# Top-k experts of a transformer layer: row gathers replaced by dense products over all 16384 experts

## What is computed

```
q = (h @ w_pq).reshape(n, 8, 2, 128)
s1 = einsum('nhd,hkd->nhk', q[:, :, 0], pk1)      # 128 keys per head
s2 = einsum('nhd,hkd->nhk', q[:, :, 1], pk2)
v1, i1 = top_k(s1, 16); v2, i2 = top_k(s2, 16)
cand = v1[..., :, None] + v2[..., None, :]        # best 16 of the 256 sums
cidx = i1[..., :, None] * 128 + i2[..., None, :]
sc, j = top_k(cand, 16); e = take_along_axis(cidx, j)
g = softmax(sc)
a = gelu(einsum('nhkd,nd->nhk', pu[e], h))        # pu, pv: [16384, 1024]
y = einsum('nhk,nhkd->nd', g * a, pv[e])
out = layer_norm(2 ** 0.25 * h + y)
```

## Time and profile before

| what | value |
|---|---|
| median of 3 runs | 4867.93 us (4850.75 to 4873.79) |
| span of the profiled execution | 4854.9 us |
| VectorE, TensorE, GpSimd, ScalarE busy | 2587.8, 3808.4, 2443.7, 821.8 us |
| software queue (the gathers) | 1107.96 MB, its packets 61.2% of 16 engines' span |
| hardware queue (all other loads and stores) | 74.99 MB, 5.1% |
| written to HBM | 6.20 MB |

### The profile page before, as it was taken

One profiled execution on the slowest core, in us unless ns is written; L12 is line 12 of the kernel. 1 busy time (PEld: TensorE's weight loads), 2 busy tenths in 40 slices (PEclk: granted clock), 3 DMA queues, 4 the chain that ended last, 5 costly groups with the idle time before them and its releaser, 6 DMA issues.

```text
span 4854.9 us, 35025 instructions
## 1 busy us (share of the span) xinstructions
PE 3808.4 (78%) x10196; PEld 1735.7 (36%) x10196; DVE 2587.8 (53%) x5932; ACT 821.8 (17%) x1886; POOL 2443.7 (50%) x2256
## 2 busy tenths in 40 slices
PE   9899898878999667888676667677778667667677
PEld 4444445545664523333222222223234222222222
DVE  0323239997214675666565465465556656445453
ACT  1210123332100111111111111111111111111111
POOL 0000000000000077777777777777777777777776
PEclk9889989987799889999999999999999999999999
DMA  2100100000210499999999999999999999999998
GB/s 82 36 2 2 55 19 20 14 7 1 70 35 27 128 340 347 354 333 332 355 364 363 366 367 360 367 372 362 362 364 388 352 355 355 359 359 353 352 368 320
DMA packets 405562, 1185.00 MB, mean 244 GB/s; under 512 B 39936, under 2 KB 125248, under 8 KB 405264
## 3 DMA queue, kind: packets, MB, share of 16 engines
q0 software_dynamic: 304384, 1107.96, 61.2%
q1 hardware_dynamic: 101008, 74.99, 5.1%
HBM read 1176.60 MB, written 6.20 MB: 244 GB/s over the span
## 4 chain that ended last, share of the span: by engine, by line
POOL 20%; DMA 17%; PE 15%; issue 9%; DVE 5%; ACT 1%; POOLq 0%; DVEq 0%; SPq 0%; ACTq 0%
DMA v_rows<-in_pv,v_rows_at 14%; PE acc L1412 11%; POOL u_rows L1351 10%; POOL v_rows L1357 9%; PE pq_ps L1379 4%; DMA u_rows<-in_pu,u_rows_at 2%; DVE u_rows L1614 1%; PE key_ps L1387 0%; DVE key_at L1507 0%; DVE one_hot L1600 0%; ACT diag L1461 0%; DVE one_hot L1596 0%; DVE key_top L1504 0%; DVE top_at L1507 0%; DVE expert_f L1602 0%
## 5 line engine op out<-in xcount | busy, mean ns | idle before, releaser
L1412 PE MATMUL acc<-v_rows,diag 128*128 128x512 f32 (+1 forms) x4224 | 2064.5, 623 | 840.6 <-DMA v_rows<-in_pv,v_rows_at 587.5
L1614 DVE CUSTOM_DVE_ANT_0 u_rows<-u_rows,late 128x1024 f32<-128x1024 f32 x1056 | 1274.2, 1226 | 1061.5 <-DMA u_rows<-in_pu,u_rows_at 1054.7
L1412 PEld LDWEIGHTS acc<-v_rows,diag 128*128 128x128 f32 (+1 forms) x4224 | 751.2, 192 | 2135.1 <-issue 1261.4
L1357 POOL DMA_INDIRECT v_rows<-in_pv,v_rows_at x1056 | 1225.1, 1160 | 325.3 <-issue 235.8
L1351 POOL DMA_INDIRECT u_rows<-in_pu,u_rows_at x1056 | 1179.8, 1117 | 369.9 <-issue 291.3
L1461 ACT ACTIVATE diag<-ident_sb,expert_w 128x128 f32<-128x128 f32 x1024 | 379.7, 397 | 1451.4 <-PE acc L1412 1364.6
L1338 POOL COPY u_rows_at<-expert 128x16 uint32<-128x16 uint32 (+1 forms) x66 | 20.2, 306 | 1193.2 <-DVE expert L1605 1180.8
L1379 PE MATMUL pq_ps<-xT_sb,w_pq_sb 128*128 128x256 f32 (+2 forms) x768 | 238.8, 465 | 8.2 <-DMA iota_sb<-in_iota 7.6
L306 POOL DMA_DIRECT2D out_gla_p<-gla_S x4 | 2.3, 587 | 480.9 <-DVE gla_S L630 480.9
L1504 DVE MAX8 key_top<-key_scores 128x8 f32<-128x128 f32 (+1 forms) x288 | 68.1, 283 | 271.2 <-ACT key_scores L1447 171.3
L930 DVE MAX8 m<-score 128x8 f32<-128x384 f32 (+6 forms) x209 | 183.4, 878 | 5.3
(11 more groups left out here) (207 smaller groups left out, 3045.9 us busy)
## 6 DMA issues: line engine op xcount, KB each, us to landing
w_pq_sb<-in_w_pq SPq DMA_DIRECT2D x48, 512.0 KB, 12.6
u_rows<-in_pu,u_rows_at POOLq DMA_INDIRECT x1056, 6.2
v_rows<-in_pv,v_rows_at POOLq DMA_INDIRECT x1056, 6.2
xT_sb<-in_xT SPq DMA_DIRECT2D x8, 528.0 KB, 7.0
w_gvr<-in_w_in SPq DMA_DIRECT2D x2, 2048.0 KB, 13.0
w_gk<-in_w_in SPq DMA_DIRECT2D x8, 512.0 KB, 6.1
w_dsa<-in_w_in SPq DMA_DIRECT2D x2, 2048.0 KB, 10.3
w_b<-in_w_in SPq DMA_DIRECT2D x8, 512.0 KB, 4.2
```

The source lines that it names most:

```text
L1357: pool.indirect_dma_start(out=V[:, j % RING, :], out_offset=None, in_=io["pv"], in_offset=bass.IndirectOffsetOnAxis(ap=atv[:, b, j:j + 1], ...
L1412: last = pe.matmul(acc[0:R, c * 512:(c + 1) * 512], dg[:, j % DG, 0:R], V[:, j % RING, c * 512:(c + 1) * 512], start=False, stop=False)
L1614: dve.tensor_tensor_reduce(U[:, j % RING, :], U[:, j % RING, :], h1[:, t, :], 1.0, 0.0, ALU.mult, ALU.add, dots[:, b, j:j + 1]).then_inc(d ...
```

## The change

`run_experts` no longer gathers. It goes over all 16384 experts for all tokens, in two passes with two scratch tensors in DRAM between them, both in float32: `gelu_rows` (128 blocks x 128 experts x 1056 tokens) and `weight_rows` (33 groups of 32 tokens x 128 x 4096). Each has 69 MB.

Pass 1 runs over 128 blocks of 128 experts. SP loads a block of `pu` in one piece (`load_block`, three buffers, each free again when TensorE has transposed it). TensorE transposes it in two halves (`turn`), ScalarE copies the halves out of PSUM, TensorE multiplies with `h1T` in three thirds of 352 tokens (`product`), ScalarE applies the gelu out of PSUM, and SP stores the 540 KB. Blocks 0 to 15 also make the queries of all tokens, one pair of head and half at a time (`query`), and blocks 1 to 16 the key scores (`keys`); VectorE takes the best 16 of all nine tiles beside that. After the picks of tile 0, block 22 transposes its numbers and weights (`turn_chosen`), so that the 128 picks of a token lie on partitions. From block 24 on, three "quads" of four tokens go beside each block, up to block 111: for each token GpSimd compares an iota with the first key numbers (`hot_key1`), VectorE with the second ones and multiplies by the weight (`hot_key2`), and TensorE multiplies the two 128x128 matrices (`weights`). That gives the token's weights of all experts; ScalarE copies four tokens at a time into one of two halves of `stage`, which SP stores as 2 MB every eight quads. The picks of the next tile go between the quads on VectorE. `early` is one SBUF buffer that holds the query data first and `stage` later.

Pass 2 is a block of its own, 32 groups of four U blocks. SP loads the gelus (`coef`), the weights (`weight_in`, in pieces of 512 bytes) and `pv`; VectorE multiplies the first two; TensorE multiplies the product with V, eight matmuls of 512 columns for each of nine tiles; VectorE adds the result to `h1` in SBUF. In the last group each tile is normalized after its add and stored by SP.

```diff
-    RING = 8
-    DG = 4
-    MAIN = TILES - 1
-    GROUPS = [[0, 1], [2, 3, 4, 5], [6, 7, 8]]
+    EB = NEXP // P
+    TC = [(0, 352), (352, 704), (704, 1056)]
+    QUADS = [r // 4 for r in ROWS]
+    NQ = sum(QUADS)
+    QAT = [sum(QUADS[:t]) for t in range(TILES)]
+    NG = NT // 32
+    KT = [[0, 1, 2, 3], [4, 5, 6, 7], [8]]
+    FIRST = 24
+    gelu_rows = nc.dram_tensor("gelu_rows", (EB, P, NT), F32, kind="Internal").ap()
+    weight_rows = nc.dram_tensor("weight_rows", (NG, P, P * 32), F32, kind="Internal").ap()
+    def quads_beside(c):
+        return [q for q in range(3 * (c - FIRST), 3 * (c - FIRST) + 3) if 0 <= q < NQ]
...
+        early = sb("early", [P, 2 * P * 32 + 512])
...
-        U = sb("u_rows", [P, RING, D])
-        V = sb("v_rows", [P, RING, D])
...
+                load_block(0)
+                load_query(0)
                 sp.dma_start(pk[:], io["pkT"]).then_inc(pk_in, 16)
                 sp.dma_start(iota[:], io["iota"]).then_inc(pk_in, 16)
...
+                load_block(1)
+                load_query(1)
+                stored = 0
+                for c in range(EB):
+                    if c + 2 < EB:
+                        load_block(c + 2)
+                    if 1 <= c and c + 1 < NB:
+                        load_query(c + 1)
+                    if c >= 1:
+                        sp.wait_ge(gelu_done, 3 * c)
+                        sp.dma_start(gelu_rows[c - 1], ga[:, (c - 1) % 3, :]).then_inc(ga_out[(c - 1) % 3], 16)
+                    while stored < NG and 8 * stored + 8 <= 3 * (c - 1 - FIRST):
+                        sp.wait_ge(w_copied, 8 * (stored + 1))
+                        sp.dma_start(weight_rows[stored], stage[:, stored % 2].rearrange("p c n -> p (c n)")).then_inc(stage_out[stored % 2], 16)
+                        stored += 1
...
+                def turn(c, half):
+                    if half == 0:
+                        pe.wait_ge(pu_in[c % 3], 16 * (c // 3 + 1))
+                    if c:
+                        pe.wait_ge(turned_copied, 2 * (c - 1) + half + 1)
+                    for b in range(4):
+                        last = pe.transpose(tps[:, half, b * P:(b + 1) * P], pu[:, c % 3, (4 * half + b) * P:(4 * half + b + 1) * P], ident[:])
+                    last.then_inc(turned, 1)
+                def product(c, s):
+                    n, (a, b) = 3 * c + s, TC[s]
+                    if s == 0:
+                        pe.wait_ge(turned_copied, 2 * c + 2)
+                    if n >= 2:
+                        pe.wait_ge(gelu_done, n - 1)
+                    for kk in range(KD):
+                        last = pe.matmul(sps[:, n % 2, 0:b - a], puT[:, c % 2, kk, :], h1T[:, kk, a:b], start=(kk == 0), stop=(kk == KD - 1))
+                    last.then_inc(s_ready, 1)
...
+                def weights(q):
+                    pe.wait_ge(hot1_built, q + 1)
+                    pe.wait_ge(hot2_built, q + 1)
+                    if q >= 2:
+                        pe.wait_ge(w_copied, q - 1)
+                    for x in range(4):
+                        last = pe.matmul(gps[:, q % 2, x * P:(x + 1) * P], oh2[:, q % 4, x, :], oh1[:, q % 4, x, :], start=True, stop=True)
+                    last.then_inc(w_ready, 1)
+                turn(0, 0)
+                turn(0, 1)
+                for c in range(EB):
+                    if c + 1 < EB:
+                        turn(c + 1, 0)
+                    if c == FIRST - 2:
+                        turn_chosen(0)
+                    for s in range(3):
+                        if c < NB:
+                            query(c, s)
+                        if 1 <= c <= NB:
+                            keys(c - 1, s)
+                        product(c, s)
+                        if s == 0 and c + 1 < EB:
+                            turn(c + 1, 1)
+                        for q in quads_beside(c)[s:s + 1]:
+                            weights(q)
+                            t = tile_of(q)
+                            if t + 1 < TILES and q == QAT[t] + 28:
+                                turn_chosen(t + 1)
+                def gelu(c, s):
+                    n, (a, b) = 3 * c + s, TC[s]
+                    act.wait_ge(s_ready, n + 1)
+                    if c >= 3 and s == 0:
+                        act.wait_ge(ga_out[c % 3], 16 * (c // 3))
+                    act.activation(ga[:, c % 3, a:b], sps[:, n % 2, 0:b - a], ACT.Gelu).then_inc(gelu_done, 1)
...
+                def copy_weights(q):
+                    k = q // 8
+                    act.wait_ge(w_ready, q + 1)
+                    if k >= 2 and q % 8 == 0:
+                        act.wait_ge(stage_out[k % 2], 16 * (k // 2))
+                    act.copy(stage[:, k % 2, :, 4 * (q % 8):4 * (q % 8) + 4],
+                             gps[:, q % 2, :].rearrange("p (x c) -> p c x", x=4)).then_inc(w_copied, 1)
...
-                            pool.indirect_dma_start(out=U[:, j % RING, :], out_offset=None, in_=io["pu"],
-                                                    in_offset=bass.IndirectOffsetOnAxis(ap=atu[:, b, j:j + 1], axis=0)).then_inc(u_in[j % RING], 16)
...
-                            pool.indirect_dma_start(out=V[:, j % RING, :], out_offset=None, in_=io["pv"],
-                                                    in_offset=bass.IndirectOffsetOnAxis(ap=atv[:, b, j:j + 1], axis=0)).then_inc(v_in[j % RING], 16)
...
+                pool.iota(count[:], [[1, P]], base=0, channel_multiplier=0, allow_small_or_imprecise_dtypes=True).then_inc(counted, 1)
+                pool.wait_ge(counted, 1)
+                for t in range(TILES):
+                    pool.wait_ge(sel_copied, t + 1)
+                    for q in range(QAT[t], QAT[t] + QUADS[t]):
+                        if q >= 4:
+                            pool.wait_ge(w_ready, q - 3)
+                        for x in range(4):
+                            n = 4 * (q - QAT[t]) + x
+                            last = pool.tensor_scalar(oh1[:, q % 4, x, :], count[:], selT[:, t % 2, 0, n:n + 1], None, ALU.is_equal)
+                        last.then_inc(hot1_built, 1)
...
-                        dve.tensor_tensor_reduce(U[:, j % RING, :], U[:, j % RING, :], h1[:, t, :], 1.0, 0.0, ALU.mult, ALU.add,
-                                                 dots[:, b, j:j + 1]).then_inc(dot_done, 1)
...
+                def hot_quad(t, q):
+                    if q >= 4:
+                        dve.wait_ge(w_ready, q - 3)
+                    for x in range(4):
+                        n = 4 * (q - QAT[t]) + x
+                        last = dve.tensor_scalar(oh2[:, q % 4, x, :], count[:], selT[:, t % 2, 1, n:n + 1], selT[:, t % 2, 2, n:n + 1],
+                                                 ALU.is_equal, ALU.mult)
+                    last.then_inc(hot2_built, 1)
+                for b in range(NB):
+                    dve.wait_ge(k_copied, 3 * (b + 1))
+                    top16(lambda x: v[:, x, b, :], lambda x: iu[:, x, b, :], lambda x: kw[:, b % 2, x, :], SAMPLE)
+                    top16(lambda x: v[0:TS, SAMPLE, b, :], lambda x: iu[0:TS, SAMPLE, b, :], lambda x: kw[0:TS, b % 2, SAMPLE, :], 1)
+                    link.wait()
+                    dve.sem_inc(top_done, 1)
+                for part in range(PH + 2):
+                    pick(0, part)
+                for t in range(TILES):
+                    dve.wait_ge(sel_copied, t + 1)
+                    for q in range(QAT[t], QAT[t] + QUADS[t]):
+                        hot_quad(t, q)
+                        part, left = divmod(q - QAT[t], 2)
+                        if t + 1 < TILES and left == 1 and part <= PH:
+                            pick(t + 1, part)
+                        if t + 1 < TILES and q == QAT[t] + 24:
+                            pick(t + 1, PH + 1)
+    GRP = EB // 4
...
+        ca = sb("coef", [P, 3, 4, NT])
+        wt = sb("weight_in", [P, 2, NG, 4, 32])
+        V = sb("pv_sb", [P, 3, 4, D])
...
+                for g in range(GRP):
+                    if g >= 3:
+                        sp.wait_ge(o_ready, TILES * (g - 2))
+                    sp.dma_start(ca[:, g % 3], gav[g]).then_inc(ca_in[g % 3], 16)
+                    if g >= 2:
+                        sp.wait_ge(c_ready, 4 * (g - 1))
+                    sp.dma_start(wt[:, g % 2].rearrange("p k c n -> p k (c n)"), wtv[g]).then_inc(wt_in[g % 2], 16)
+                    sp.dma_start(V[:, g % 3], pvv[g]).then_inc(V_in[g % 3], 16)
+                    if g == 1:
+                        sp.dma_start(gain, io["ln2_g"].to_broadcast([P, D])).then_inc(ln_in, 16)
+                        sp.dma_start(offset, io["ln2_b"].to_broadcast([P, D])).then_inc(ln_in, 16)
...
+            @block.tensor
+            def _(pe):
+                for g in range(GRP):
+                    pe.wait_ge(c_ready, 4 * (g + 1))
+                    pe.wait_ge(V_in[g % 3], 16 * (g // 3 + 1))
+                    for t in range(TILES):
```

(56 more changed lines are left out.)

551 lines of the change are left out of this document (198 added, 353 removed).

## The result

The changed kernel takes 6074.57 us (median of 4 runs, 6064.53 to 6085.92), the kernel before 4868.31 in the same comparison (4850.75 to 4873.79). The ratio is 1.2476, with an interval of 1.2438 to 1.2513. The forecast was 3970, faster, with a range to 4200. It was wrong by 2100 us and on the wrong side.

A forecast was written before the change was run, and what follows sets the result against it. It took the old expert stage as bound by gather bytes and the new one by PE: start 1602.4, pass 1 to 2907, turnover 23, 31 groups 958, last group 63.7, end 2.4, 13 outside the span: 3970 µs, range 3910 to 4200.

The forecast's parts named there:

- the price of a matmul: PE in both passes: 24 matmuls of 352 columns 7.10 µs, 32 of 512 columns 13.74; PE's floor 2257 µs.
- the charge of 20: Pass 1: 20 µs together (0 to 60) for POOL and DVE locking, the `stage` margin and nine ACT function table exchanges.
- That TensorE paces both passes: Both passes: PE work of 1267.9 µs and 989 µs sets the time; PE over 95% busy from 1602 to the turnover.
- Stores run like loads: Pass 1 DMA: 199 GB/s is covered if stores reach the rate of loads, 376 GB/s in 4 KB rows.
- Rival 3: Scratch stores pace pass 1: 4015 µs at 200 GB/s, 4755 at 79; chance 0.10 together with slow reads.
- The strided weight copy on ACT: Pass 1, three per block: no row shows it; 2.2 µs each would fill the block, so nothing was charged.
- Turnover: Between pass 1 and pass 2: last gelu, its store, first loads and four products leave PE idle for 23 µs.
- Clock after a wait: PE at 1.2 GHz for a part: 2 µs each at the start, after block 22 and at pass 2, 6 together.
- Stall at block 22: Pass 1: PE waits at `turn_chosen(0)` for DVE's picks of the first tile, 13 µs (0 to 20).
- Tail: Last group of pass 2: DVE adds and normalizes nine tiles at 6.70 µs each, 63.7 in all, twice PE's time.
- POOL's price: Pass 1, `hot_key1`: 0.3 µs for each of 1056 `tensor_scalar` of 128 elements; POOL paces quads only above 0.77.
- POOL beside DVE: Pass 1 quads: POOL loses up to one DVE operation per issue, at worst 6.2 of 6.2 µs per two quads.

The follow-up runs named there:

- `half_all`: The changed kernel with half of the U products, half of the query products and half of pass 2's products left out: 4100.02 us.
- `uv_bf16`: The changed kernel with the products of both passes in bfloat16; queries, keys and one-hot products stay float32: 3426.1 us, timed 3433.14, ratio 0.7048 to the kernel before.

## Why the prediction was wrong, step by step

**The step that failed: the price of a matmul.** The forecast put "24 matmuls of 352 columns: from 1285.99 to 1293.09, that is 7.10 µs. One U block is exactly that (`product`, 3 thirds x 8)." The 7.10 us were right and the 24 are records, of 12 matmuls. All prices but that of the transposes were taken that way, and each is wrong by the same factor. Measured beside forecast, in us:

| term | forecast | by two records a matmul | shown |
|---|---|---|---|
| U products, 128 | 908.8 | 1817.6 | half of them is worth 906 |
| `query`, 16 | 113.6 | 227.2 | 16 records a third |
| `keys` | 15.8 | 31.6 | 8 records for 4 matmuls, 0.89 |
| `weights`, 264 quads | 116.2 | 232.3 | 8 records, 0.89 a quad |
| transposes (`turn`, `turn_chosen`) | 113.5 | 113.5 (one record) | 4 in 0.44 |
| pass 1, PE | 1267.9 | 2422.2 | 2438.6 (1600.15 to about 4038.8) |
| pass 2, PE | 989 | 1977.6 | 1989.9 |

With these the forecast's path is 1602.4 + 2422.2 + 6 of clock + 23 of turnover + 1977.6 + about 9 behind the last matmul (DVE's last tile and its store) + 13 outside the span: 6053, 0.4% under the measured 6074.6. This sum is made after the result: the 9 us are measured, and the charge of 20 and the stall of 13 are left out, of which the trace shows 3.2. The same two records turn up in the kernel before, so the time of each row was read rightly, and only the number of matmuls in it was not. The forecast's last doubt, "if matmuls with these operands run slower than the rows I priced them from", is not what happened. A record runs here at the speed of the rows; the count was wrong.

The Trainium skill has the rule that would have raised the question: "FP8 and Floating Point Precision", section "TensorE Precision Notes", puts true FP32 at four passes through the PE array. The trace agrees in time, 4.74 us against 1.19 for the same eight matmuls in bfloat16, 3.98 times; it shows not four records but two, each of twice the length of a bfloat16 one.

What the factor did to the decision: TensorE's floor of 4400 us plus 1602 lies above the old 4868 by itself. For the new stage to match the old one, PE's work had to stay under 3263 us, less turnover and tail. A count of the loops against the rows would have turned the forecast round.

**What held, and what only looked so.**
- *That TensorE paces both passes*: shown, by two cuts that gave back 906 and 962 us.
- *Stores run like loads*: shown. 528 KB land in 2.9 us and 2 MB in 8.2, that is 186 and 256 GB/s by themselves; the 79 GB/s of the `y` store went beside the gathers, and no large store here is as slow. Rival 3 falls: neither in `half_all` nor in `uv_bf16`, whose blocks with quads take 8.0 us, did an engine wait for a store.
- *The strided weight copy on ACT* costs the price of an ordinary one: 585 ns, 586 in the earlier trace rows.
- *Turnover*: 24.9 us (23 forecast).
- *Clock after a wait*: 16 records took 6.49 us from 1600.15 to 1606.64, at a granted clock of 0.73 after PE had mostly waited at 0.50 (1.2 GHz); the next 16 take 4.74 at 1.00. That is the 2 us of the earlier trace rows.
- *Stall at block 22*: 3.2 us in the changed kernel, 7.7 in the two kernels with half the products of pass 1 (13 forecast), 30.2 in `uv_bf16`. The forecast's cause, DVE late with its picks, is seen in those three. In the changed kernel DVE had its picks ready early, and it was ACT that came late: `soften(0)` stands behind the gelus of block 21 in ACT's list, so DVE waited 35.0 us for it. First DVE, then PE:

```profile
2200.39 0.28 DVE L1491 TENSOR_REDUCE total<-top 128x8 f32<-128x128 f32 x1 [35.02 <-ACT top L1375]
```

```profile
2201.29 0.90 PE L1295 MATMUL key_ps<-ident_sb,chosen 128*128 128x128 f32 x3 [3.18 <-DVE chosen L1495]
```

- *Tail*: sized 63.7 because DVE's nine tiles were to outlast PE's 30.9. PE's last group takes about 62 (1989.9 / 32) and DVE keeps up, so 9 us are left behind the last matmul. In `half_all` DVE's tiles do end the last group, 6.75 us apart (6.70 forecast).
- *POOL's price*: mis-sized, 0.3 forecast, 0.686 measured in the mean. It stays under the 0.77 named as its limit, 2.74 us of the 3.10 of a quad at the forecast pace. `half_all`, at 3.55 a quad, shows no wait for it; in bfloat16 it does pace the quads.

**POOL beside DVE** was the mechanism that the forecast charged at 20 us. It is real, with its size in the changed kernel's timeline of POOL and DVE:

```profile
2654.35 2.42 POOL L1412 TENSOR_SCALAR hot_key<-count,chosenT 128x128 f32<-128x128 f32 x4 [2.07 <-PE weight_ps L1304]
2659.98 3.55 POOL L1412 TENSOR_SCALAR hot_key<-count,chosenT 128x128 f32<-128x128 f32 x4 [3.20 <-PE weight_ps L1304]
...
2661.01 0.98 DVE L1466 TENSOR_TENSOR one_hot<-iota_sb,top_at_f 128x800 f32<-128x800 f32 x1
2662.02 1.04 DVE L1469 TENSOR_TENSOR one_hot<-one_hot,cand_e 128x800 f32<-128x800 f32 x1
```

Four rows take 2.42 us beside DVE's `hot_key2` alone and 3.55 when DVE's two `one_hot` operations with two inputs run into them: 1.13 more, about one DVE operation. But beside the `tensor_scalar` rows of DVE POOL takes 0.60 each, its minimum being 0.59. So the loss behind the `tensor_scalar`s that the forecast feared (8 x 0.227) does not show here. The Trainium skill says in "SBUF — State Buffer", section "Who interferes with whom", that a DVE instruction with two SBUF inputs contends with a GpSimd instruction that reads SBUF, and that a `tensor_scalar` can where it runs in a two-port mode. The trace agrees on the first, with 3.55 against 2.42 us; beside these rows it shows nothing of the second. Its figure in "GPSIMD Engine Reference", section "Performance versus the Vector engine", gave an estimate of 0.4 in all; the trace has 0.60 undisturbed.

What stays open: why POOL needs 0.60 us for 128 elements. It does not fall with the bytes written (681 ns in the mean for both types); whether its fixed part or its loop is the dear one was not measured.

## What to carry to other kernels

Before a row becomes a price, count what the program issues at that line and divide the row's count by it: a row of 24 float32 matmuls was 12, and the whole forecast hung on it. When a change moves work to TensorE, ask next in which type it runs there. The same change lost 25% in float32 and won 31% with the operands of both passes and the stored gelus in bfloat16, and then POOL's small rows and the transfers, both covered before, became the limits. The bfloat16 kernels round these operands; how far that moves the output is not shown here.

## What the hardware showed

- A float32 matmul is two weight loads and two matmul records: 4.74 us for 8 matmuls of 352 columns, 0.86 for one of 512, 0.84 ns for each column and record. In bfloat16 it is one of each: 1.19 us for the 8, and 0.22 for one of 512. That is a quarter of the float32 time. A float32 transpose with `ident` is one record of 128 columns, 0.11 us.
- POOL needs 0.60 us for a row of 128 elements that DVE starts every 0.20 to 0.26 us; four rows take 2.42 us, and 3.55 when two two-input operations of DVE run beside them.
- Loads reached 363 GB/s in pass 2 of the bfloat16 kernel, with TensorE busy 362 of 400 us and a third of the bytes in pieces of 512, where the gathers of the earlier trace rows reached 361.
